# Encoder trunk kernel: a prologue in single token tiles, with the squares of x behind the operand splits

## The chip, the cores and the metric

The kernel runs on one core of a Trainium2 chip. Its time is the device time of one execution, in microseconds (us), and the number that counts is the median of several executions. A trace comes from one further execution under the hardware profiler. The engines are named as in the profile: PE is TensorE (PEld its weight load), DVE is VectorE, ACT is ScalarE, POOL is GpSimd, SP is SyncE, the engine that issues every DMA here. Each engine works through its own instructions in order and waits on semaphores for the others.

## The reference

Two layers over 1088 token rows (a prompt of 1024 and a sample of 64) with a width of 1024. The part that the change touches is the head of the first layer: an RMS norm and the projection `w_in`.

```python
def rmsnorm(x, g):
    xf = x.astype(jnp.float32)
    xf = xf * lax.rsqrt(jnp.mean(xf * xf, axis=-1, keepdims=True) + RMS_EPS)
    return xf.astype(x.dtype) * g
...
    z = rmsnorm(x, norm_g) @ w_in
...
    x = x + mixed @ lp['w_out']
    y, conv_state = conv_ffn(x, lp['ffn_norm'], lp['w_up'], lp['conv_w'], lp['conv_b'], lp['w_down'], conv_buf)
    x = x + y
```

Between them stand three mixers (a gated MLP, a windowed attention and a matrix memory), behind them a convolutional feed-forward block; all of this is the same before and after the change.

## The kernel before

**Tiles.** x lies in HBM by rows of tokens. `TOK` cuts it into nine token tiles: 0 to 7 are 128 prompt rows each, 8 is the sample. `CH` groups three of them into a chunk: 384, 384 and 322 columns once x is turned. On chip x is held turned, as `xT` (128 partitions by 8 blocks of the width by tokens). Every fp32 product is made of three products of a split operand: `split3` (lines 321 to 325) multiplies high by high, low by high and high by low. So x times the norm's gain is split into `actH` (ACT, `norm_high`, line 434) and `actL` (DVE, `norm_low`, line 440), and the weights into `wzH` (ACT) and `wzL` (DVE), `split_wz0`, lines 1397 and 1993, in four pieces of 512 KB: pieces 0 and 1 are the halves of weight group 0, pieces 2 and 3 of group 1.

**The norm's factor comes late.** The products run on x times the gain alone. The factor of each token, `rt`, is applied when ACT takes a finished unit out of PSUM (`evac_z`, line 1429, with the Gelu function). `rt` comes from three steps: ACT squares a tile of x with a running sum (`xsq`, line 1389, semaphore `vs_r`), DVE scales the sums of three tiles (`norm_mean`, line 394), and POOL raises them to the power of -1/2 (`norm_power`, line 400, semaphore `rt_r`).

**The prologue.** SP issues the loads in one row: ident, x tiles 0 to 2, five small rows of gains (`grows`), weight pieces 0 and 1, x tile 3, piece 2, x tile 4, piece 3, then the other tiles. Tiles 7 and 8 share a buffer with 0 and 1, and wait for `vs_r` of those. PE does 12 transposes that feed nobody (`fill`), turns tiles 0 to 2 (`turn_x`, line 882; 8 transposes each), turns the gains, and does 28 more fills. ACT and DVE each copy half of a turned tile to `xT` (lines 1391 and 1988, semaphores `xin_ea` and `xin_ev`). ACT squares each tile before it copies its half. Then come the splits of chunk 0.

**The units.** PE then works through units of `z_products`: a unit is one token tile by 256 columns of `w_in`, 24 matmuls. Unit 0 is tile 0 with group 0, units 1 and 2 are tiles 1 and 2 with group 0, unit 3 is tile 0 with group 1. Behind units 0, 1 and 2 PE turns tiles 3, 4 and 5, behind 4, 5 and 6 the tiles 6, 7 and 8. Since all tiles from 3 on use the same PSUM banks 4 and 5, the turn of tile t waits until both halves of tile t - 1 have been copied out (`xin_ea` and `xin_ev` at least t). ACT's order there is: evacuate unit 0, square and copy tile 3, evacuate unit 1, square and copy tile 4, and so on.

```python
                if t >= 3:
                    pe.wait_ge(xin_ea, t)
                    pe.wait_ge(xin_ev, t)
...
                    act.wait_ge(rt_r, norm_at(2 * l, t // 3) + 1)
                    act.activation(zst[0:r, u % 3, 0:w], bank[z_bank(u)][0:r, 0:w],
                                   ACT.Gelu if u < 18 else ACT.Copy, scale=rt[0:r, t:t + 1]).then_inc(z_ev, 1)
```

Of the kernel before, what the change touches and what calls it, by code (L numbers as in the profile page):

```python
# [7 lines left out]
F32 = mybir.dt.float32  # L8
F32R = mybir.dt.float32r
ALU = mybir.AluOpType  # L10
ACT = mybir.ActivationFunctionType
# [3 lines left out]
P = 128  # L15
D = 1024
KT = D // P
# [12 lines left out]
TOK = [(i * P, P) for i in range(NB)] + [(SOFF, DEC)]  # L30
# [58 lines left out]
def build(nc, I, O):  # L89
# [11 lines left out]
    with ctx:  # L101
# [4 lines left out]
        xT = sb("xT", [P, KT, TC])  # L106
# [224 lines left out]

        def act_at(n, c):

            return n // 2 * 32 + (24 if n % 2 else c * KT)

        def ms_at(n, c):
            return n * 4 + (1, 2, 4)[c]
# [46 lines left out]
        def norm_mean(dve, n, c):  # L384
            if n == 2 * DEPTH and c == 2:
                src = vs[:, 0:3]
            elif n:
                dve.wait_ge(ssq_mm, norm_at(n - 1, c) + 1)
                src = sum_bank(n, c)[:, SS:SS + 3]
            else:  # L390
                dve.wait_ge(vs_r, 3 * c + 3)
                src = vs[:, 3 * c:3 * c + 3]
            k = 2 if c == 2 else 3
            dve.tensor_scalar(ms[:, 3 * c:3 * c + k], src[:, 0:k], 1.0 / D, EPS, ALU.mult, ALU.add).then_inc(ms_r, 1)
            if c == 2:
                dve.tensor_scalar(ms[0:DEC, NB:NB + 1], src[0:DEC, 2:3], 1.0 / D, EPS, ALU.mult, ALU.add).then_inc(ms_r, 1)
# [35 lines left out]
        def norm_high(act, n, c, m):  # L432
            t0, w = CH[c]
            act.activation(actH[:, m, t0:t0 + w], xT[:, m, t0:t0 + w], ACT.Copy,
                           scale=gains[:, n * KT + m:n * KT + m + 1]).then_inc(act_h, 1)

        def norm_low(dve, n, c, m):
            t0, w = CH[c]
# [153 lines left out]
        def _(sp):  # L592
# [3 lines left out]
            def load_x(t):  # L596
                if t >= 7:
                    sp.wait_ge(xin_tp, t - 6)
                    sp.wait_ge(vs_r, t - 6)
                sp.dma_start(xin[0:TOK[t][1], t % 7], I["x_sample"][0] if t == NB else xp[t]).then_inc(xin_in[t % 7], 16)  # L600

            def load_wz(l, s, piece=None):

                g = z_group(s)
                w = ZG[1] if g == 8 else ZG[0]
                k0, k1 = (0, KT) if piece is None else (4 * piece, 4 * piece + 4)
                w_in = I["w_in"][l].rearrange("(k p) n -> p k n", p=P)
                sp.dma_start(rawz(s, l)[:, k0:k1, 0:w], w_in[:, k0:k1, g * ZG[0]:g * ZG[0] + w]).then_inc(
                    rz_in if piece is None else rz0_in[2 * s + piece], 16)

            for t in range(3):
                load_x(t)
            for n, (name, l) in enumerate([(f"{part}_norm", l) for l in range(DEPTH) for part in ("attn", "ffn")]):
                sp.dma_start(grows[n * KT:(n + 1) * KT, :], I[name][l].rearrange("(a b) -> a b", b=P)).then_inc(rows_in, 16)
            sp.dma_start(grows[2 * DEPTH * KT:, :], I["final_norm"].rearrange("(a b) -> a b", b=P)).then_inc(rows_in, 16)
            load_wz(0, 0, 0)
            load_wz(0, 0, 1)
            load_x(3)
            load_wz(0, 1, 0)
# [250 lines left out]
        def _(pe):  # L870
            pe.wait_ge(const_in, 16)

            def turn_x(t):

                r = TOK[t][1]
                b = 2 * t if t < 3 else 4
                pe.wait_ge(xin_in[t % 7], 16 * (t // 7 + 1))
# [3 lines that stand above are left out]
                for k in range(KT):  # L881
                    m = pe.transpose(bank[b + k // 4][:, (k % 4) * P:(k % 4) * P + r],
                                     xin[0:r, t % 7, k * P:(k + 1) * P], ident[0:r, 0:r])
                m.then_inc(xin_tp, 1)

            def fill(count):

                for _ in range(count):
                    pe.transpose(bank[6][:, 0:P], ident[:, :], ident[:, :])

            fill(12)
            for t in range(3):
                turn_x(t)
            n = (2 * DEPTH + 1) * KT
            pe.wait_ge(rows_in, (2 * DEPTH + 1) * 16)
            pe.transpose(bank[7][:, 0:n], grows[0:n, :], ident[0:n, 0:n]).then_inc(rows_tp, 1)
            fill(28)
            pe.wait_ge(s_ones, 3)

            for l in range(DEPTH):  # L900
                M0, F0 = l * MMS, l * FREES

                def z_products(u):

                    s, _, w, t = z_unit(u)
                    t0, r = TOK[t]
                    if u >= 18:
                        pe.wait_ge(wz_l, l * 16 + wz_at(s))
                    if u < 4:
                        if l:  # L910
                            pe.wait_ge(bank_free, l * FREES - 7 + u)
                    elif u < ZB + 2:
                        pe.wait_ge(z_ev, l * ZU + u - 3)
                    else:
                        pe.wait_ge(z_ev, l * ZU + u - 1)
                    if u in (6, 12):
                        pe.wait_ge(act_l, act_at(2 * l, u // 6) + KT)
                    out = bank[z_bank(u)][0:r, 0:w]
                    for k in range(KT):
                        if u in (0, 3) and k % 4 == 0:  # L920
                            pe.wait_ge(wz_l, l * 16 + 2 * s + k // 4 + 1)
                        if u == 0:
                            pe.wait_ge(act_l, act_at(2 * l, 0) + k + 1)
                        m = split3(pe, out, actH[:, k, t0:t0 + r], actL[:, k, t0:t0 + r],
                                   wzH[s % 2][:, k, 0:w], wzL[s % 2][:, k, 0:w], k == 0, k == KT - 1)
                    m.then_inc(z_mm, 1)
# [453 lines left out]

        @block.scalar
        def _(act):
            def turn_x(t):
                t0, r = TOK[t]
                b = 2 * t if t < 3 else 4
                act.wait_ge(xin_in[t % 7], 16 * (t // 7 + 1))
                if t:
                    act.wait_ge(vs_r, t)
                act.activation(xsq[0:r, :], xin[0:r, t % 7], ACT.Square, accum_out=vs[0:r, t:t + 1]).then_inc(vs_r, 1)
                act.wait_ge(xin_tp, t + 1)  # L1390
                act.activation(xT[:, 0:4, t0:t0 + r], bank[b][:, :].rearrange("p (k t) -> p k t", k=4)[:, :, 0:r],
                               ACT.Copy).then_inc(xin_ea, 1)

            def split_wz0(l, j):
                s, k = j // 2, 4 * (j % 2)
                act.wait_ge(rz0_in[j], (l + 1) * 16)
                act.activation(wzH[s][:, k:k + 4, 0:ZG[0]], rawz(s, l)[:, k:k + 4, 0:ZG[0]], ACT.Copy).then_inc(wz_h, 1)

            for t in range(3):
                turn_x(t)  # L1400
            act.wait_ge(rows_tp, 1)
            act.activation(gains[:, :], bank[7][:, 0:(2 * DEPTH + 1) * KT], ACT.Copy).then_inc(gains_r, 1)
            act.wait_ge(gains_r, 1)
            act.wait_ge(xin_ea, 3)
            act.wait_ge(xin_ev, 3)
            for m in range(KT):
                norm_high(act, 0, 0, m)
                if m in (1, 3):
                    split_wz0(0, m // 2)
            split_wz0(0, 2)  # L1410
            split_wz0(0, 3)

            for l in range(DEPTH):
                M0, F0 = l * MMS, l * FREES
# [568 lines left out]
        def _(dve):  # L1983
            def turn_x(t):
                t0, r = TOK[t]
                b = 2 * t if t < 3 else 4
                dve.wait_ge(xin_tp, t + 1)
                dve.tensor_copy(xT[:, 4:8, t0:t0 + r], bank[b + 1][:, :].rearrange("p (k t) -> p k t", k=4)[:, :, 0:r]).then_inc(xin_ev, 1)

            def split_wz0(l, j):  # L1990
                s, k = j // 2, 4 * (j % 2)
                dve.wait_ge(wz_h, l * 16 + j + 1)
                dve.tensor_tensor(wzL[s][:, k:k + 4, 0:ZG[0]], rawz(s, l)[:, k:k + 4, 0:ZG[0]],
                                  wzH[s][:, k:k + 4, 0:ZG[0]].bitcast(F32), ALU.subtract).then_inc(wz_l, 1)

            dve.memset(xT[:, :, SEQ:SOFF], 0.0)
            for c in range(3):
                for t in range(3 * c, 3 * c + 3):
                    turn_x(t)
                if c == 0:  # L2000
                    dve.wait_ge(s_ones, 3)
                    dve.wait_ge(gains_r, 1)
                norm_mean(dve, 0, c)
                for m in range(KT):
                    norm_low(dve, 0, c, m)
                    if c == 0 and m in (1, 3):
                        split_wz0(0, m // 2)
                if c == 0:
                    split_wz0(0, 2)
                    split_wz0(0, 3)  # L2010

            for l in range(DEPTH):
                M0, F0 = l * MMS, l * FREES
# [556 lines left out]
```

## Time and profile before

| | us |
|---|---|
| median of 3 executions | 2484.2 (2484.17 to 2485.09) |
| the profiled execution | 2480.56 |
| its span, first to last instruction | 2478.7 |

The span is cut into the busy time of each engine, the waits (idle time of an engine, put down to what ended it), and the chain of work that ended last, which is followed back from the last instruction. The profiled execution is 3.6 us shorter than the median of the others; what lies around its span is 1.9 us. A timeline merges instructions that follow each other into one row, with their count; one that ends with a bracket tells how long the engine was idle before it and what ended that.

### The profile page before, as it was taken

How to read it: one execution, taken by the hardware profiler on the slowest of the kernel's cores; microseconds unless marked ns; L12 is line 12 of the kernel's file. 1: busy time of each engine (PE TensorE's matmuls, PEld its weight loads, DVE VectorE, ACT ScalarE, POOL GpSimd, SP SyncE). 2: the span in 40 equal slices, each digit the busy share in tenths (PEclk: the TensorE clock that was granted, in tenths of full speed). 3: DMA queues.
4: the chain of work that ended last, by engine and by line, in shares of the span. 5: the costliest groups of instructions: out<-in, count | busy, mean ns of one | idle time of the engine just before them, and what ended most of it. 6: DMA issues, size and time to landing. Idle time of an engine off the chain costs nothing.

```text
span 2478.7 us, 41939 instructions
## 1 busy us (share of the span) xinstructions
PE 2442.6 (99%) x16587; PEld 2377.1 (96%) x16587; DVE 1603.5 (65%) x2715; ACT 1096.6 (44%) x2069; POOL 537.1 (22%) x498
## 2 busy tenths in 40 slices
PE   9999999999999999999999999999999999999999
PEld 8999888999999999999999988889999999999999
DVE  3115688888888887464611266879888888864554
ACT  6325656543433333343433356655343333333453
POOL 0001253432222220010110112444322222200110
PEclk9999999999999999999999999999999999999999
DMA  4443322122222223654524333212122222245564
GB/s 153 132 133 95 114 82 77 54 64 68 79 73 75 79 65 112 199 170 162 196 71 143 110 109 115 82 49 71 62 78 75 73 79 66 74 155 180 176 193 149
DMA packets 238071, 265.89 MB, mean 107 GB/s; under 512 B 15638, under 2 KB 207924, under 8 KB 235700
## 3 DMA queue, kind: packets, MB, share of 16 engines
q1 hardware_dynamic: 237876, 263.22, 33.4%
q8 instruction: 132, 2.16, 0.4%
q14 instruction: 63, 0.52, 0.1%
HBM read 213.06 MB, written 50.11 MB: 106 GB/s over the span
## 4 chain that ended last, share of the span: by engine, by line
PE 88%; DVE 5%; issue 3%; ACT 2%; DMA 1%; POOL 0%; SPq 0%; DVEq 0%; POOLq 0%; ACTq 0%
PE bank L323 27%; PE bank L325 26%; PE bank L324 26%; PE bank L1042 2%; PE bank L1115 1%; PE bank L1084 1%; PE bank L1100 1%; PE bank L1125 1%; PE bank L1064 1%; PE bank L1076 0%; DVE actL L2239 0%; PE bank L995 0%; DMA rawB<-in_w_down 0%; DVE cv L2342 0%; DVE tL L2239 0%
## 5 line engine op out<-in xcount | busy, mean ns | idle before, releaser
L323 PE MATMUL bank<-actH,wb 128*128 128x384 f32 (+1 forms) x1768 | 578.5, 327 | 1.7 <-DVE xT L2036 1.7
L324 PE MATMUL bank<-actL,wb 128*128 128x384 f32 (+1 forms) x1768 | 573.0, 324 | 0.0
L325 PE MATMUL bank<-actH,wb 128*128 128x384 f32 (+1 forms) x1768 | 572.5, 324 | 0.0
L323 PE MATMUL bank<-wzH,actH 128*128 128x256 f32 (+3 forms) x1296 | 369.2, 285 | 2.2 <-DVE actL L440 1.1
L325 PE MATMUL bank<-wzH,actL 128*128 128x256 f32 (+3 forms) x1296 | 364.2, 281 | 0.0
L324 PE MATMUL bank<-wzL,actH 128*128 128x256 f32 (+3 forms) x1296 | 363.8, 281 | 0.0
L323 PEld LDWEIGHTS bank<-actH,wb 128*128 128x128 f32 x1768 | 332.9, 188 | 7.1 <-issue 6.1
L324 PEld LDWEIGHTS bank<-actL,wb 128*128 128x128 f32 x1768 | 333.7, 189 | 0.7
L325 PEld LDWEIGHTS bank<-actH,wb 128*128 128x128 f32 x1768 | 333.8, 189 | 0.0
L323 PEld LDWEIGHTS bank<-wzH,actH 128*128 128x128 f32 (+1 forms) x1296 | 236.3, 182 | 5.1 <-issue 3.0
L323 PE MATMUL bank<-tH,wb 128*128 128x384 f32 x704 | 236.6, 336 | 1.2 <-ACT vn L1788 1.2
L324 PEld LDWEIGHTS bank<-wzL,actH 128*128 128x128 f32 (+1 forms) x1296 | 236.5, 182 | 0.0
L324 PE MATMUL bank<-tL,wb 128*128 128x384 f32 x704 | 236.3, 336 | 0.0
L325 PE MATMUL bank<-tH,wb 128*128 128x384 f32 x704 | 236.3, 336 | 0.0
L325 PEld LDWEIGHTS bank<-wzH,actL 128*128 128x128 f32 (+1 forms) x1296 | 236.1, 182 | 0.0
L1681 ACT ACTIVATE cv<-upb,convc 128x1090 f32<-128x1090 f32 x88 | 114.5, 1301 | 246.3 <-DVE upb L2329 246.1
L2352 DVE TENSOR_TENSOR wb<-raw,wb 128x1024 fp32r<-128x1024 f32 x88 | 107.7, 1224 | 168.5 <-ACT wb L1697 168.3
L2307 DVE TENSOR_TENSOR upb<-bank,upb 128x384 f32<-128x384 f32 x294 | 155.4, 552 | 65.1 <-PE bank L325 62.1
L1659 ACT ACTIVATE Sx<-Sf 128x512 fp32r<-128x512 f32 x168 | 105.3, 628 | 207.8 <-POOL Sf L1952 207.8
L1952 POOL TENSOR_TENSOR Sf<-raw 128x512 f32<-128x512 f32 x84 | 116.6, 1388 | 359.4 <-PE bank L325 355.9
L1429 ACT ACTIVATE zst<-bank,stat 128x256 f32<-128x256 f32 (+3 forms) x162 | 75.8, 472 | 240.1 <-PE bank L325 239.8
L1697 ACT ACTIVATE wb<-raw 128x1024 fp32r<-128x1024 f32 x88 | 93.1, 1060 | 197.5 <-PE bank L325 159.8
(303 smaller groups left out, 5066.6 us busy)
## 6 DMA issues: line engine op xcount, KB each, us to landing
raw<-in_w_up SPq DMA_DIRECT2D x88, 512.0 KB, 4.2
raw<-in_w_down SPq DMA_DIRECT2D x88, 512.0 KB, 3.6
g_scratch<-cv SPq DMA_DIRECT2D x44, 545.0 KB, 3.2
rawz<-in_w_in SPq DMA_DIRECT2D x22, 1024.0 KB, 5.4
zb<-z_scratch SPq DMA_DIRECT2D x16, 1156.0 KB, 5.6
tHf<-g_scratch SPq DMA_DIRECT2D x88, 192.0 KB, 3.6
z_scratch<-zst SPq DMA_DIRECT2D x128, 128.0 KB, 1.7
raw<-in_w_out SPq DMA_DIRECT2D x128, 128.0 KB, 2.9
```

Source lines behind the costliest of these rows:

```text
L323: pe.matmul(out, aH, bH, start=first, stop=False)
L324: pe.matmul(out, aH, bL, start=False, stop=False)
L325: return pe.matmul(out, aL, bH, start=False, stop=last)
L1042: m = pe.matmul(bank[2 * c + p // 2][64 * v:64 * v + 64, (p % 2) * 256 + k0:(p % 2) * 256 + k1], bqT[64 * v:64 * v + 64, p, 64 * c:64 * c ...
L1064: pe.matmul(bank[6][:, 0:4 * r], ones[0:r, :], dA[0:r, 0:4 * r], start=True, stop=True).then_inc(S["A_r"], 1)
L1429: act.activation(zst[0:r, u % 3, 0:w], bank[z_bank(u)][0:r, 0:w], ACT.Gelu if u < 18 else ACT.Copy, scale=rt[0:r, t:t + 1]).then_inc(z_ev, 1)
L1659: act.activation(Sx[:, s, 0], Sf[:, s, 1], ACT.Copy).then_inc(s_h, 1)
L1681: act.activation(cv[:, :], (upb2 if h else upb1)[:, PAD:], ACT.Identity, scale=convc[:, f + 88:f + 89], bias=convc[:, f + 132:f + 133]).th ...
L1697: act.activation(h, t, ACT.Copy).then_inc(w_h, 1)
L1952: pool.tensor_tensor(Sf[:, s, 1], x, y, ALU.add if s == 0 else ALU.subtract).then_inc(s_r, 1)
L2307: dve.tensor_tensor(out, bank[b][:, 0:out.shape[1]], other, ALU.mult if i in (6, 9) else ALU.add).then_inc(take_r, 1)
L2352: dve.tensor_tensor(lo, t, h.bitcast(F32), ALU.subtract).then_inc(w_l, 1)
```

## The change

The prologue is written anew in single tiles. The layers' loops are as they were.

- SP: x tile 0, then the gains, then weight piece 0, then x tiles 1 and 2, then piece 1. The rest follows as before.
- PE: turns tile 0, then the gains, 8 fills, tiles 1 and 2, 4 fills. Unit 0 waits for the low parts of tile 0 alone, unit 1 for those of tiles 1 and 2.
- ACT and DVE: the split of x comes in 8 instructions on the 128 columns of tile 0 (`FIRST`) and 8 on the 256 columns of tiles 1 and 2 (`OTHERS`), where it was 8 on 384 columns. The copies of tiles 1 and 2 and the splits of weight pieces 0 and 1 stand between them.
- ACT: the squares of tiles 0, 1 and 2 stand behind all splits, where each stood ahead of its tile's copy. DVE's `norm_mean` of chunk 0 stands behind the splits too.
- `act_at` counts eight increments more, since chunk 0 has 16 splits now.

```diff
--- before.py
+++ after.py
@@ -331,7 +331,7 @@
 
         def act_at(n, c):
 
-            return n // 2 * 32 + (24 if n % 2 else c * KT)
+            return KT + n // 2 * 32 + (24 if n % 2 else c * KT)
 
         def ms_at(n, c):
             return n * 4 + (1, 2, 4)[c]
@@ -434,6 +434,17 @@
             act.activation(actH[:, m, t0:t0 + w], xT[:, m, t0:t0 + w], ACT.Copy,
                            scale=gains[:, n * KT + m:n * KT + m + 1]).then_inc(act_h, 1)
 
+        FIRST, OTHERS = slice(0, P), slice(P, 384)
+
+        def first_high(act, m, cols):
+
+            act.activation(actH[:, m, cols], xT[:, m, cols], ACT.Copy, scale=gains[:, m:m + 1]).then_inc(act_h, 1)
+
+        def first_low(dve, m, cols):
+            dve.wait_ge(act_h, (KT if cols is OTHERS else 0) + m + 1)
+            dve.scalar_tensor_tensor(actL[:, m, cols], xT[:, m, cols], gains[:, m:m + 1], actH[:, m, cols].bitcast(F32),
+                                     ALU.mult, ALU.subtract).then_inc(act_l, 1)
+
         def norm_low(dve, n, c, m):
             t0, w = CH[c]
             dve.wait_ge(act_h, act_at(n, c) + m + 1)
@@ -608,12 +619,13 @@
                 sp.dma_start(rawz(s, l)[:, k0:k1, 0:w], w_in[:, k0:k1, g * ZG[0]:g * ZG[0] + w]).then_inc(
                     rz_in if piece is None else rz0_in[2 * s + piece], 16)
 
-            for t in range(3):
-                load_x(t)
+            load_x(0)
             for n, (name, l) in enumerate([(f"{part}_norm", l) for l in range(DEPTH) for part in ("attn", "ffn")]):
                 sp.dma_start(grows[n * KT:(n + 1) * KT, :], I[name][l].rearrange("(a b) -> a b", b=P)).then_inc(rows_in, 16)
             sp.dma_start(grows[2 * DEPTH * KT:, :], I["final_norm"].rearrange("(a b) -> a b", b=P)).then_inc(rows_in, 16)
             load_wz(0, 0, 0)
+            load_x(1)
+            load_x(2)
             load_wz(0, 0, 1)
             load_x(3)
             load_wz(0, 1, 0)
@@ -889,12 +901,14 @@
                     pe.transpose(bank[6][:, 0:P], ident[:, :], ident[:, :])
 
             fill(12)
-            for t in range(3):
-                turn_x(t)
+            turn_x(0)
             n = (2 * DEPTH + 1) * KT
             pe.wait_ge(rows_in, (2 * DEPTH + 1) * 16)
             pe.transpose(bank[7][:, 0:n], grows[0:n, :], ident[0:n, 0:n]).then_inc(rows_tp, 1)
-            fill(28)
+            fill(8)
+            turn_x(1)
+            turn_x(2)
+            fill(4)
             pe.wait_ge(s_ones, 3)
 
             for l in range(DEPTH):
@@ -919,7 +933,9 @@
                     for k in range(KT):
                         if u in (0, 3) and k % 4 == 0:
                             pe.wait_ge(wz_l, l * 16 + 2 * s + k // 4 + 1)
-                        if u == 0:
+                        if u == 0 and l == 0:
+                            pe.wait_ge(act_l, k + 1)
+                        elif u == 1 - min(l, 1):
                             pe.wait_ge(act_l, act_at(2 * l, 0) + k + 1)
                         m = split3(pe, out, actH[:, k, t0:t0 + r], actL[:, k, t0:t0 + r],
                                    wzH[s % 2][:, k, 0:w], wzL[s % 2][:, k, 0:w], k == 0, k == KT - 1)
@@ -1380,13 +1396,18 @@
 
         @block.scalar
         def _(act):
-            def turn_x(t):
-                t0, r = TOK[t]
-                b = 2 * t if t < 3 else 4
+            def square_x(t):
+                r = TOK[t][1]
                 act.wait_ge(xin_in[t % 7], 16 * (t // 7 + 1))
                 if t:
                     act.wait_ge(vs_r, t)
                 act.activation(xsq[0:r, :], xin[0:r, t % 7], ACT.Square, accum_out=vs[0:r, t:t + 1]).then_inc(vs_r, 1)
+
+            def turn_x(t):
+                t0, r = TOK[t]
+                b = 2 * t if t < 3 else 4
+                if t > 2:
+                    square_x(t)
                 act.wait_ge(xin_tp, t + 1)
                 act.activation(xT[:, 0:4, t0:t0 + r], bank[b][:, :].rearrange("p (k t) -> p k t", k=4)[:, :, 0:r],
                                ACT.Copy).then_inc(xin_ea, 1)
@@ -1396,19 +1417,28 @@
                 act.wait_ge(rz0_in[j], (l + 1) * 16)
                 act.activation(wzH[s][:, k:k + 4, 0:ZG[0]], rawz(s, l)[:, k:k + 4, 0:ZG[0]], ACT.Copy).then_inc(wz_h, 1)
 
-            for t in range(3):
-                turn_x(t)
+            turn_x(0)
             act.wait_ge(rows_tp, 1)
             act.activation(gains[:, :], bank[7][:, 0:(2 * DEPTH + 1) * KT], ACT.Copy).then_inc(gains_r, 1)
+            split_wz0(0, 0)
             act.wait_ge(gains_r, 1)
+            act.wait_ge(xin_ea, 1)
+            act.wait_ge(xin_ev, 1)
+            for m in range(4):
+                first_high(act, m, FIRST)
+            turn_x(1)
+            for m in range(4, KT):
+                first_high(act, m, FIRST)
+            split_wz0(0, 1)
+            turn_x(2)
             act.wait_ge(xin_ea, 3)
             act.wait_ge(xin_ev, 3)
             for m in range(KT):
-                norm_high(act, 0, 0, m)
-                if m in (1, 3):
-                    split_wz0(0, m // 2)
+                first_high(act, m, OTHERS)
             split_wz0(0, 2)
             split_wz0(0, 3)
+            for t in range(3):
+                square_x(t)
 
             for l in range(DEPTH):
                 M0, F0 = l * MMS, l * FREES
@@ -1994,20 +2024,28 @@
                                   wzH[s][:, k:k + 4, 0:ZG[0]].bitcast(F32), ALU.subtract).then_inc(wz_l, 1)
 
             dve.memset(xT[:, :, SEQ:SOFF], 0.0)
-            for c in range(3):
+            turn_x(0)
+            dve.wait_ge(s_ones, 3)
+            dve.wait_ge(gains_r, 1)
+            split_wz0(0, 0)
+            for m in range(4):
+                first_low(dve, m, FIRST)
+            turn_x(1)
+            for m in range(4, KT):
+                first_low(dve, m, FIRST)
+            split_wz0(0, 1)
+            turn_x(2)
+            for m in range(KT):
+                first_low(dve, m, OTHERS)
+            split_wz0(0, 2)
+            split_wz0(0, 3)
+            norm_mean(dve, 0, 0)
+            for c in range(1, 3):
                 for t in range(3 * c, 3 * c + 3):
                     turn_x(t)
-                if c == 0:
-                    dve.wait_ge(s_ones, 3)
-                    dve.wait_ge(gains_r, 1)
                 norm_mean(dve, 0, c)
                 for m in range(KT):
                     norm_low(dve, 0, c, m)
-                    if c == 0 and m in (1, 3):
-                        split_wz0(0, m // 2)
-                if c == 0:
-                    split_wz0(0, 2)
-                    split_wz0(0, 3)
 
             for l in range(DEPTH):
                 M0, F0 = l * MMS, l * FREES
```

On ACT, from its split of chunk 0 to the copy of x tile 3. Before (`rz0_in2` and `rz0_in3` are the landings of weight pieces 2 and 3, `z_mm` is a finished unit):

```order
L434 ACTIVATE actH<-xT,gains 128x384 [waits xin_ev,xin_ea,gains_r]
L434 ACTIVATE actH<-xT,gains 128x384
L1397 ACTIVATE wzH<-rawz 128x4x256 [waits rz0_in0]
L434 ACTIVATE actH<-xT,gains 128x384 x2
L1397 ACTIVATE wzH<-rawz 128x4x256 [waits rz0_in1]
L434 ACTIVATE actH<-xT,gains 128x384 x4
L1397 ACTIVATE wzH<-rawz1a 128x1024 [waits rz0_in2]
L1397 ACTIVATE wzH<-rawz1a 128x1024 [waits rz0_in3]
L1429 ACT_TABLE_LOAD [waits rt_r]
L1429 ACTIVATE zst<-bank,stat 128x256 [waits z_mm]
L1389 ACTIVATE xsq,stat<-xin 128x1024 [waits vs_r,xin_in3]
L1391 ACTIVATE xT<-bank 128x4x128 [waits xin_tp]
```

and after, on ACT, from the split of weight piece 1:

```order
L1418 ACTIVATE wzH<-rawz 128x4x256 [waits rz0_in1]
L1412 ACTIVATE xT<-bank 128x4x128 [waits xin_tp]
L441 ACTIVATE actH<-xT,gains 128x256 [waits xin_ev,xin_ea]
L441 ACTIVATE actH<-xT,gains 128x256 x7
L1418 ACTIVATE wzH<-rawz1a 128x1024 [waits rz0_in2]
L1418 ACTIVATE wzH<-rawz1a 128x1024 [waits rz0_in3]
L1404 ACTIVATE xsq,stat<-xin 128x1024 [waits xin_in0]
L1404 ACTIVATE xsq,stat<-xin 128x1024 [waits vs_r,xin_in1]
L1404 ACTIVATE xsq,stat<-xin 128x1024 [waits vs_r,xin_in2]
L1459 ACT_TABLE_LOAD [waits rt_r]
L1459 ACTIVATE zst<-bank,stat 128x256 [waits z_mm]
L1404 ACTIVATE xsq,stat<-xin 128x1024 [waits vs_r,xin_in3]
```

The three squares of chunk 0 have moved from the front of ACT's row to the place between the last weight split and the table load of unit 0's evacuation.

On DVE, the same place in the program. Before:

```order
L1988 COPY xT<-bank 128x4x128 [waits xin_tp] x3
L394 TENSOR_SCALAR stat<-stat 128x3 [waits vs_r,gains_r,s_ones]
L440 SCALAR_TENSOR_TENSOR actL<-xT,gains,actH 128x384 [waits act_h] x2
L1993 TENSOR_TENSOR wzL<-rawz,wzH 128x4x256 [waits wz_h]
L440 SCALAR_TENSOR_TENSOR actL<-xT,gains,actH 128x384 [waits act_h] x2
L1993 TENSOR_TENSOR wzL<-rawz,wzH 128x4x256 [waits wz_h]
L440 SCALAR_TENSOR_TENSOR actL<-xT,gains,actH 128x384 [waits act_h] x4
L1993 TENSOR_TENSOR wzL<-rawz1a,wzH 128x1024 [waits wz_h] x2
```

and after:

```order
L2018 COPY xT<-bank 128x4x128 [waits xin_tp]
L2023 TENSOR_TENSOR wzL<-rawz,wzH 128x4x256 [waits wz_h,gains_r,s_ones]
L445 SCALAR_TENSOR_TENSOR actL<-xT,gains,actH 128x128 [waits act_h] x4
L2018 COPY xT<-bank 128x4x128 [waits xin_tp]
L445 SCALAR_TENSOR_TENSOR actL<-xT,gains,actH 128x128 [waits act_h] x4
L2023 TENSOR_TENSOR wzL<-rawz,wzH 128x4x256 [waits wz_h]
L2018 COPY xT<-bank 128x4x128 [waits xin_tp]
L445 SCALAR_TENSOR_TENSOR actL<-xT,gains,actH 128x256 [waits act_h] x8
L2023 TENSOR_TENSOR wzL<-rawz1a,wzH 128x1024 [waits wz_h] x2
L394 TENSOR_SCALAR stat<-stat 128x3 [waits vs_r]
```

DVE's copies of tiles 1 and 2, which stood together ahead of every split, now each wait behind a split of weights or of x, and `norm_mean` (line 394) has gone from the front to the end.

## Rows read from the trace of the kernel before

**Rows 1.** The page: the span, and PE's busy time, share and instructions.
```profile
span 2478.7 us, 41939 instructions
PE 2442.6 (99%) x16587; PEld 2377.1 (96%) x16587; DVE 1603.5 (65%) x2715; ACT 1096.6 (44%) x2069; POOL 537.1 (22%) x498
```

**Rows 2.** Timeline of PE, first units and turns: start us, us, line, operation, tiles.
```profile
16.64 0.36 PE L323 MATMUL bank<-wzH,actH 128*128 128x256 f32 x1 [1.12 <-DVE actL L440]
...
18.60 1.03 PE L882 MATMUL bank<-ident,xin 128*128 128x128 f32 x8
...
22.30 1.04 PE L882 MATMUL bank<-ident,xin 128*128 128x128 f32 x8
```

**Rows 3.** Timeline of ACT, from the first copy to the copy of x tile 3.
```profile
6.67 0.60 ACT L1391 ACTIVATE xT<-bank 128x512 f32<-128x512 f32 x1 [1.01 <-PE bank L882]
...
10.20 0.21 ACT L1402 ACTIVATE gains<-bank 128x40 f32<-128x40 f32 x1
...
16.40 1.99 ACT L1397 ACTIVATE wzH<-rawz1a 128x1024 fp32r<-128x1024 f32 x2
18.41 1.28 ACT L1429 ACT_TABLE_LOAD   x1
19.70 0.47 ACT L1429 ACTIVATE zst<-bank,stat 128x256 f32<-128x256 f32 x1
20.07 1.05 ACT L1389 ACTIVATE xsq<-xin 128x1024 f32<-128x1024 f32 x1
21.02 0.19 ACT L1389 ACTIVATION_READ_ACCUMULATOR xsq<-xin 128x1 f32 x1
21.11 0.59 ACT L1391 ACTIVATE xT<-bank 128x512 f32<-128x512 f32 x1
```

**Rows 4.** Timeline of SP: the issues of the first loads.
```profile
1.19 1.37 SPq L600 DMA_DIRECT2D xin<-in_x_prompt  x3
...
4.02 0.29 SPq L615 DMA_DIRECT2D grows<-in_final_norm  x1
4.35 0.95 SPq L608 DMA_DIRECT2D rawz<-in_w_in  x2
```

**Rows 5.** DMA issues, us to landing: x tile 0, weight pieces 0 and 1.
```profile
xin<-in_x_prompt SPq DMA_DIRECT2D x1, 512.0 KB, 3.3
...
rawz<-in_w_in SPq DMA_DIRECT2D x1, 512.0 KB, 5.6
...
rawz<-in_w_in SPq DMA_DIRECT2D x1, 512.0 KB, 6.5
```

**Rows 6.** Timeline of ACT: eight high parts at 384 and at 322 columns.
```profile
30.27 4.15 ACT L434 ACTIVATE actH<-xT,gains 128x384 fp32r<-128x384 f32 x8
...
44.41 3.74 ACT L434 ACTIVATE actH<-xT,gains 128x322 fp32r<-128x322 f32 x8
```

**Rows 7.** Timeline of DVE: a weight split, and the copy of a tile.
```profile
14.74 1.22 DVE L1993 TENSOR_TENSOR wzL<-rawz,wzH 128x1024 fp32r<-128x1024 f32 x1
...
20.27 0.69 DVE L1988 COPY xT<-bank 128x512 f32<-128x512 f32 x1
```

**Rows 8.** Timeline of three engines: from the last square of chunk 1 to its factor.
```profile
27.53 0.19 ACT L1389 ACTIVATION_READ_ACCUMULATOR xsq<-xin 128x1 f32 x1
...
27.75 0.17 DVE L394 TENSOR_SCALAR stat<-stat 128x3 f32<-128x3 f32 x1
...
28.00 0.85 POOL L400 TENSOR_TENSOR stat<-stat 128x3 f32<-128x3 f32 x1 [16.32 <-DVE stat L394]
```

**Rows 9.** Waits of PE, longest first: what for, us in total, times, longest.
```profile
PE bank L323 <- DVE Sx L2235: 8.5, 2, 4.3
```

**Rows 10.** Stretches around the first of them: length, PE busy (instructions), granted clock, DMA share, GB/s.
```profile
514.00:516.00 2.00, 0.00 (x0) 1.00 0.00 0
516.00:518.00 2.00, 0.23 (x1) 0.96 0.00 0
...
519.00:520.00 1.00, 1.00 (x5) 0.50 0.07 16
...
521.00:522.00 1.00, 1.00 (x6) 0.87 0.00 0
522.00:523.00 1.00, 1.00 (x8) 1.00 0.00 0
```

## Prediction

> **What bounds the kernel now.** I read the page first: PE is busy for 99% of the span [rows 1]. So the time is PE's work plus its few waits, and an edit of the prologue can only move the point from which PE runs without a stop. That point is read from PE's timeline. Its last wait of the prologue ends at 16.64 us, where unit 0 had waited for low parts of x, and from there units and turns follow each other: tile 3 is turned at 18.60, tile 4 at 22.30 [rows 2]. Unit 0 is thus done at 18.60 and unit 1 at 22.30. The row at 22.30 is my yardstick: whatever the change does ahead of it, everything behind it is the same work in the same order on every engine, so the kernel's time moves by as much as that row moves (plus what the clock adds, below).
>
> Two things must be there for the turn of tile 4. One is PE itself, done with units 0 and 1. The other is ACT: it must have copied tile 3, and ahead of that copy stand, in its order, all splits, the table load, the evacuation of unit 0 and the square of tile 3. ACT's timeline shows that chain before: splits to 18.39, table load at 18.41, evacuation at 19.70, square at 20.07, its sum at 21.02, copy at 21.11, done at 21.70 [rows 3]. The slack against PE's 22.30 was only 0.6 us. That is the number to look at, since the change puts work on this chain.
>
> **The gain on PE's side.** Tile 0's own splits are smaller and stand first, so unit 0 can be done earlier. I build the times below: unit 0 ends near 16.5 instead of 18.60, and unit 1 waits for the `OTHERS` parts and ends near 19.5 instead of 22.30. By this alone 2.8 us would be won.
>
> **ACT's chain after the change, step by step.**
> - Start. The first square used to run while PE turned tile 0. Now ACT has nothing before the copy at 6.67 [rows 3], since fills and tile 0 come as before. Copy and gains take 0.5 and 0.2: 7.4.
> - Weight piece 0. Its issue stood at 4.35, behind two tiles of x [rows 4], and it landed 5.6 later, at 9.95 [rows 5]. Now it follows tile 0 and five small issues, near 3.4. With little ahead of it it should take tile 0's 3.3 [rows 5]: 6.7, at most a us more. I take a start of 7.4, one split's pitch is 1.0 (two in 1.99, [rows 3]): 8.4.
> - Tile 0's high parts. Eight at 384 columns took 4.15, 0.52 each, eight at 322 took 3.74, 0.47 each [rows 6]: 0.83 ns for a column, so 0.31 at 128 columns and 0.41 at 256. Four: 9.6. Copy of tile 1, 0.5: 10.1 (its turn is done by then if it lands by 9; two of 512 KB stand ahead of it). Four more: 11.3.
> - Weight piece 1 had landed at 4.80 + 6.5 = 11.3 [rows 4, 5]; four tiles of 512 KB stand ahead of it now as then, with a pause in the issues for the gains. I take 11.5, up to 12.2. High part: 12.55.
> - Now the cross wait. ACT must wait for DVE's copy of tile 2 (`xin_ev`), which stands behind DVE's split of piece 1. That takes 1.14 to the next instruction's start (1.22 long), the copy 0.69 [rows 7]: 12.6 + 1.14 + 0.69 = 14.45.
> - `OTHERS`, eight at 0.41: 17.75. Pieces 2 and 3, 1.95: 19.7. So the splits are done 1.3 later than before, though they began sooner: sixteen instructions cost 5.8 where eight cost 4.15, and ACT stands still for about 1.5 at the cross wait.
> - The three squares. Square and sum take 1.14 (20.07 to 21.21, [rows 3]), and each waits for the sum before it: 3 x 1.17 = 3.5, to 23.2. Before, all this was at the front, where half of it was hidden by PE's transposes.
> - The factor. From the end of the last sum to the factor's end took 27.72 to 28.85, 1.13, through DVE and POOL [rows 8]: 24.35. Before, nobody waited for it. Now the table load has the wait on `rt_r` ahead of it, so it starts only then: 1.29 to the evacuation's start [rows 3], 25.65. Then as before 1.41 from the evacuation to the copy's start and 0.59 for the copy [rows 3]: 27.65.
>
> So the turn of tile 4 starts at 27.7, and 27.7 - 22.3 = **5.4 us later**. PE's gain is eaten entirely: PE would stand still from 19.5 to 27.7. Queued behind the same wait are, on SP, the loads of tiles 7 and 8, which wait for `vs_r`; they would leave near 21 and are turned after 40, so they cost nothing. DVE's `norm_mean` holds up its copy of tile 3, but only to 24, less than ACT's.
>
> **The clock.** The trace has a stall of such a size: PE idle for 4.3 us, for DVE's Sx [rows 9]. Around its end the granted clock falls to half, that is from 2.4 to 1.2 GHz. The stretches give 0.04 x 2 x 2 = 0.16, three full microseconds, and 0.26: 3.4 us at the lower level [rows 10]. At half rate these do 1.7 us of work, and by instructions (5 a us against 8) the loss is 1.3. A stall of 8 us is longer than that, so I expect it again, and take 1.6. From both sides: nothing if the clock stays, and twice the 1.3, 2.7, if PE starts at the lower level and has to work through a second such stretch. The waits of 1.1 us in the prologue of before show no such price [rows 2], but a stall of 8 us is near to the one of 4.3, not to those.
>
> Sum: 5.4 + 1.6 = +7.0. The profiled execution would go from 2480.56 to 2487.6; against the median of 2484.2, which is 3.6 above it, the same difference gives **2491.2**. A shift as a whole is right because no engine behind unit 2 has work that waits for anything but this chain.
>
> The switch of ACT's table is where a page speaks. In the row the load takes 1.28, and the evacuation starts 0.01 behind it. The Trainium skill (ScalarE: Activation LUTs, What ACT_TABLE_LOAD costs) gives about 1.28 us for the load and another 1.38 for a drain. By it, an estimate from that page, the sum would be 1.4 higher, since the switch is now on the path; the trace shows no drain behind the load, and I keep the row's figure.
>
> **Rivals.**
> - *The table load is not held.* If ACT loads the table as soon as the squares are issued, the load lies beside DVE and POOL, and 1.1 of it is saved: +5.9, 2490.1. For it: before, it started 0.02 behind the split. Against: it has the wait on `rt_r`, which had long been met then.
> - *The clock stays.* +5.4, 2489.6. For it: short waits leave it alone. Against: [rows 10].
> - *The table switch costs more.* If ACT has to empty first, with its factor just in, a switch could cost its length twice: +8.3, 2492.5. The row at 19.70 speaks against it.
> - *The other side: PE is what decides.* If ACT's chain came through by 19.5, the turn of tile 4 would start when unit 1 ends, and the kernel would win 2.8: 2481.4. It decides from the point where the copy of tile 3 is done by 19.5; ACT's work alone, from 6.67 on with no wait, is 0.7 + 4 x 1.0 + 5.8 + 2 x 0.5 + 3.5 = 15.0, which ends at 21.7 ahead of the factor, so it needs squares or splits far cheaper than their rows. Between it and the forecast lies the case that waits and splits are cheaper by a us or so in sum and the clock stays: +3 to +5, within 0.2%.
>
> **How the numbers follow.** Forecast as worked out, with steps off by up to a us: 0.64. Load not held: 0.11. Clock stays with the stall as forecast: 0.09. Switch dearer: 0.03. Chain shorter, within 0.2%: 0.10. PE decides: 0.03, also within 0.2%. About 0.2%, 5 us, is what a measurement of this kernel can tell from no change, so the line is at 2489.2. Some of the cases that end above it in the mean (clock stays, load not held) spill over it by 0.03 together. Faster gets 0.01, for what no case covers. That makes faster 0.01, same 0.10 + 0.03 + 0.03 - 0.01 = 0.15, slower 0.84. The range: down to a stall as forecast without the clock's price, 2489.2, and up to piece 1 landing at 12.2 (+0.7) with the clock's dear end (+1.1), 2493.0.
>
> **What the profile after would show.** The turn of tile 4 at 27.7 with an idle time ahead of it of some 8 us, put down to ACT's or DVE's copy; the splits of pieces 2 and 3 done near 19.7; squares from there to 23.2; the factor near 24.4; the table load behind it, not beside it; a granted clock of 0.5 for some 3.4 us around 28. Unit 0 would run in two halves, with a wait for the low part of piece 1 between them. The forecast is wrong if the copy of tile 3 ends before 24, or if the load starts ahead of the factor.

## Result, and the profile after

| | before | after |
|---|---|---|
| median of 7 executions each, us | 2484.17 (2479.72 to 2485.09) | 2491.29 (2489.12 to 2494.29) |
| profiled execution, us | 2480.56 | 2491.29 |
| its span, us | 2478.7 | 2489.5 |

The ratio is 1.0034, with a 95% interval from 1.0023 to 1.0045: the changed kernel is slower by 0.34%, 7.1 us between the medians. The forecast was 2491.2. The profiled executions stand further apart, by 10.8 us (the forecast for the changed kernel's was 2487.6); where these come from is taken up below.

The page of the changed kernel shows the same busy shares, and a first slice (of 62 us) in which PE is no longer busy all the time:

```profile
span 2489.5 us, 41924 instructions
PE 2446.0 (98%) x16571; PEld 2380.9 (96%) x16571; DVE 1602.2 (64%) x2723; ACT 1099.3 (44%) x2077; POOL 537.2 (22%) x498
...
PE   7999999999999999999999999999999999999999
```

The waits of PE over the whole changed kernel (what for, us in total, times, longest) have a new first row. The second is the one that stood first before, [rows 9]:

```profile
PE bank L894 <- ACT xT L1412: 8.7, 1, 8.7
PE bank L323 <- DVE Sx L2273: 8.5, 2, 4.3
```

PE's timeline puts that wait in front of the turn of x tile 4. These rows answer to [rows 2]: the second half of unit 0 starts at 13.74 after its wait for the low part of weight piece 1 (16.64 before, for a low part of x), tile 3 is turned at 15.27 instead of 18.60, tile 4 at 27.79 instead of 22.30. The 8 transposes take 1.94 us instead of 1.04, and tile 5 is turned at 33.91, which is 6.1 behind tile 4.

```profile
13.74 0.39 PE L323 MATMUL bank<-wzH,actH 128*128 128x256 f32 x1 [0.95 <-DVE wzL L2023]
15.27 1.04 PE L894 MATMUL bank<-ident,xin 128*128 128x128 f32 x8
27.79 1.94 PE L894 MATMUL bank<-ident,xin 128*128 128x128 f32 x8 [8.65 <-ACT xT L1412]
33.91 1.03 PE L894 MATMUL bank<-ident,xin 128*128 128x128 f32 x8
```

ACT's timeline of the same stretch answers to [rows 3]. It can be read from the bottom: the copy of tile 3 at 27.10 is behind its square (26.07), that behind the evacuation of unit 0 (25.69), that behind the table load (24.40), that behind the factor (POOL, a wait of 1.29), and that behind three squares from 19.50 on:

```profile
12.33 0.58 ACT L1412 ACTIVATE xT<-bank 128x512 f32<-128x512 f32 x1
14.38 3.31 ACT L441 ACTIVATE actH<-xT,gains 128x256 fp32r<-128x256 f32 x8 [1.47 <-DVE xT L2018]
17.60 1.99 ACT L1418 ACTIVATE wzH<-rawz1a 128x1024 fp32r<-128x1024 f32 x2
19.50 1.04 ACT L1404 ACTIVATE xsq<-xin 128x1024 f32<-128x1024 f32 x1
...
22.92 0.19 ACT L1404 ACTIVATION_READ_ACCUMULATOR xsq<-xin 128x1 f32 x1
24.40 1.28 ACT L1459 ACT_TABLE_LOAD   x1 [1.29 <-POOL stat L400]
25.69 0.47 ACT L1459 ACTIVATE zst<-bank,stat 128x256 f32<-128x256 f32 x1
26.07 1.05 ACT L1404 ACTIVATE xsq<-xin 128x1024 f32<-128x1024 f32 x1
...
27.10 0.59 ACT L1412 ACTIVATE xT<-bank 128x512 f32<-128x512 f32 x1
```

The stretches of the changed kernel (length, PE busy, granted clock) show what the stall did to TensorE's clock. It fell to half, that is from 2.4 to 1.2 GHz, while PE was idle, and came back only between 32 and 34 us, some 5 us after PE had work again:

```profile
22.00:24.00 2.00, 0.00 (x0) 0.68 0.78 270
24.00:26.00 2.00, 0.00 (x0) 0.50 0.32 98
...
28.00:30.00 2.00, 2.00 (x11) 0.50 0.19 66
30.00:32.00 2.00, 2.00 (x11) 0.50 0.00 0
32.00:34.00 2.00, 2.00 (x15) 0.76 0.00 0
34.00:36.00 2.00, 2.00 (x20) 1.00 0.20 66
```

A landmark further down is ACT's next table load, behind unit 17. It stands at 72.81 before (the first row) and at 80.73 after (the second), 7.9 later:

```profile
72.81 1.28 ACT L1449 ACT_TABLE_LOAD   x1
80.73 1.28 ACT L1479 ACT_TABLE_LOAD   x1
```

The later turn of tile 4 makes 5.5 of it (27.79 - 22.30). The other 2.4 I put down to the clock; the first experiment tests that. I use this landmark for all kernels below, since nothing that the variants edit stands behind it.

### The profile page after: what moved, and what is told of

Read it like the earlier page. It is cut to its first block, busy times and chain, and to the rows that moved or that the text cites. A ratio compares the mean times of both kernels' runs of the same rounds, so it can differ in the third digit from the quotient of the medians.

```text
span 2489.5 us, 41924 instructions
## 1 busy us (share of the span) xinstructions
PE 2446.0 (98%) x16571; PEld 2380.9 (96%) x16571; DVE 1602.2 (64%) x2723; ACT 1099.3 (44%) x2077; POOL 537.2 (22%) x498
## 4 chain that ended last, share of the span: by engine, by line
PE 87%; DVE 6%; issue 3%; ACT 2%; DMA 1%; POOL 1%; SPq 0%; DVEq 0%; POOLq 0%; ACTq 0%
PE bank L323 27%; PE bank L325 26%; PE bank L324 26%; PE bank L1058 1%; PE bank L1131 1%; DMA zb<-z_scratch 1%; PE bank L1100 1%; PE bank L1116 1%; PE bank L1141 1%; DVE hc L2213 1%; DVE actL L2277 1%; PE bank L1080 1%; PE bank L1092 0%; DMA rawB<-in_w_down 0%; PE bank L1011 0%
```

## Experiments

Each was timed beside the kernel before, unless said otherwise, and profiled once. Single profiles differ by some tenths of a us in when x and the weights land (in those of the changed kernel's variants the split of weight piece 0 starts between 7.3 and 8.2), so a share read from two of them is taken as good to about 0.5 us, an estimate from these starts.

**The clock taken out.** 76 transposes that feed nobody, into a bank that is free there, fill PE's wait:

```diff
                     z_products(u)
                     if l == 0:
+                        if u == 1:
+                            fill(76)
                         if u in (0, 1, 2):
                             turn_x(3 + u)
```

> The changed kernel with 76 more fill transposes on PE between unit 1 and the turn of tile 4, at 0.109 us each 8.3 us, inside its wait of 8.65 us. If the clock is what costs beyond the wait: the turn of tile 4 stays at 27.8, no row shows a granted clock of 0.5 there, the turn of tile 5 starts 3.7 us behind that of tile 4 instead of 6.1, and the median is 2.4 us under the changed kernel's, near 2488.9. Rival, that unit 2 was slow for another reason (a port shared with ACT and DVE): the 6.1 us stay and the median is 2491.3.

Measured: PE's timeline has the fills from 19.49 on, and tile 5's turn 3.8 behind tile 4's, instead of 6.1. The last two rows are stretches: with the fills the granted clock stays at 1.00.

```profile
19.49 8.46 PE L901 MATMUL bank<-ident 128*128 128x128 f32 x76
28.30 1.06 PE L894 MATMUL bank<-ident,xin 128*128 128x128 f32 x8 [0.36 <-issue]
32.06 1.04 PE L894 MATMUL bank<-ident,xin 128*128 128x128 f32 x8
...
26.00:28.00 2.00, 1.95 (x18) 1.00 0.19 65
28.00:30.00 2.00, 1.70 (x15) 1.00 0.20 66
```

Tile 4's turn is 0.5 later here, for a first tile and weights that landed later. The landmark is at 78.84, 6.0 behind the kernel before, which is the 6.0 by which tile 4's turn is late (28.30 - 22.30) and nothing for the clock. Median 2489.85, ratio 1.0027 (1.0016 to 1.0037). So the clock's share of the changed kernel is 2.4 us, and the rival of a slow unit 2 is out. The medians don't show it: 2489.85 is 7.2 above the kernel before timed beside it (2482.66), and the changed kernel was 7.1 above its own. The trace is what shows it.

**The squares back in front.** The changed kernel, with each square ahead of its tile's copy, and `norm_mean` ahead of the last weight splits on DVE:

```diff
...
             def turn_x(t):
...
-                if t > 2:
-                    square_x(t)
+                square_x(t)
...
             split_wz0(0, 2)
             split_wz0(0, 3)
-            for t in range(3):
-                square_x(t)
...
+            norm_mean(dve, 0, 0)
             split_wz0(0, 2)
             split_wz0(0, 3)
-            norm_mean(dve, 0, 0)
```

> The changed kernel with each square ahead of its tile's copy again, and norm_mean ahead of the splits of weight pieces 2 and 3; order of loads, splits by tile and fills stay as changed. If the squares and the factor behind the splits make the wait: splits of pieces 2 and 3 done near 20.5, factor long there, table load beside nothing but at once, turn of tile 4 near 23.9 instead of 27.8, median 2485 to 2487.5. Rival, that the doubled number of splits and the wait of ACT for DVE's copy of tile 2 carry most of it: the turn of tile 4 after 26 and a median of 2490.

Measured: ACT's table load follows the splits at once, and PE's turn of tile 4 starts at 23.97.

```profile
18.57 1.99 ACT L1417 ACTIVATE wzH<-rawz1a 128x1024 fp32r<-128x1024 f32 x2
20.58 1.28 ACT L1455 ACT_TABLE_LOAD   x1
...
23.97 1.94 PE L894 MATMUL bank<-ident,xin 128*128 128x128 f32 x8 [3.87 <-ACT xT L1411]
```

Median 2487.51, ratio 1.0018 (1.0009 to 1.0027); landmark at 75.91, 3.1 behind the kernel before. The place of the squares and the factor carries 3.8 of the 5.5 us of the stall, and the rest of the change, with more and smaller splits and the wait for DVE, carries 1.7 of its own (some 0.2 of it is a later start: the split of weight piece 0 is at 7.54 here, at 7.32 in the changed kernel). A wait of 3.9 is enough for the lower clock: the 8 transposes again take 1.94.

**The table load out from behind the factor.** One line behind the third square:

```diff
             for t in range(3):
                 square_x(t)
+            act.preload_act_table_set("gelu_and_others")
```

> The changed kernel with the load of the Gelu table right behind the third square, where it waits for nothing, beside norm_mean and the power. If the load is on the path because it stands behind the wait for the factor: the evacuation of unit 0 starts near 24.5 and the turn of tile 4 near 26.6, 1.15 earlier than 27.8; the median 1.1 us under the changed kernel's (2490.1). Rival, that the load is hidden anyway: the turn of tile 4 at 27.8.

Measured: ACT loads the table while DVE and POOL make the factor.

```profile
23.36 1.28 ACT L1442 ACT_TABLE_LOAD   x1
24.66 0.47 ACT L1460 ACTIVATE zst<-bank,stat 128x256 f32<-128x256 f32 x1
...
26.76 1.94 PE L894 MATMUL bank<-ident,xin 128*128 128x128 f32 x8 [7.38 <-ACT xT L1412]
```

The evacuation follows 0.02 behind the load, and the turn of tile 4 is at 26.76; from the start of the last square to the copy's start it is now 3.87, against 5.14 in the changed kernel. The landmark (79.12) is 1.6 earlier. The load was on the path by its place behind the wait. The median doesn't show it: 2490.95, ratio 1.0032 (1.0019 to 1.0044), where 2490.1 was expected.

**The squares alone.** The kernel before, with nothing but the squares of tiles 0 to 2 and `norm_mean` moved behind the splits:

```diff
...
+            for t in range(3):
+                square_x(t)
...
-                norm_mean(dve, 0, c)
+                if c:
+                    norm_mean(dve, 0, c)
...
                     split_wz0(0, 2)
                     split_wz0(0, 3)
+                    norm_mean(dve, 0, 0)
```

> The kernel before with one part of the change alone: squares of tiles 0 to 2 and norm_mean behind the splits. If the place of the squares makes most of the wait: splits done near 18.0, squares to 21.5, factor 22.7, table load behind it, turn of tile 4 near 26.0 instead of 22.3; +3.7, and up to 2.4 more if the clock falls: 2487.9 to 2490.3. Rival, that the squares merely fill idle time of ACT: the turn of tile 4 stays within 0.5 us of 22.3, 2484.2.

Measured: unit 0 and the turn of tile 3 are about where they were (18.36 against 18.60), and the turn of tile 4 waits.

```profile
22.96 1.28 ACT L1436 ACT_TABLE_LOAD   x1 [1.29 <-POOL stat L400]
...
26.35 1.94 PE L882 MATMUL bank<-ident,xin 128*128 128x128 f32 x8 [4.13 <-ACT xT L1396]
```

Median 2489.95, ratio 1.0028 (1.0018 to 1.0038); landmark at 78.38, 5.6 behind the kernel before. From this side too the move of the squares is worth 4.1 us of stall, and 1.5 for the clock.

**The copies ahead.** If the stall is only for the copies of x, the copies can go first. ACT takes its half of tile 3 ahead of the splits of weight piece 2, tile 4's behind piece 3, tile 5's behind the squares; DVE likewise:

```diff
...
+            turn_x(3)
             split_wz0(0, 2)
             split_wz0(0, 3)
+            turn_x(4)
             for t in range(3):
                 square_x(t)
+            turn_x(5)
...
                         if u in (1, 2, 3):
-                            turn_x(u + 2)
+                            square_x(u + 2)
```

> The changed kernel with the copies of tiles 3, 4 and 5 (both halves) taken out of the row behind the evacuations: tile 3's ahead of the splits of weight piece 2, tile 4's behind those of piece 3, tile 5's behind the squares; their squares stay where they were. If the wait is for the copy alone: the turn of tile 4 starts when unit 1 is done, near 19.3, with no wait of 8 us and no half clock. Then ACT is late next: unit 4 waits for the first evacuation near 27.3, and the turn of tile 7 for the copy of tile 6, behind chunk 1's high parts, near 38 (36.41 in the kernel before). Median 1 to 2 us over the kernel before: 2484 to 2485. Rival, that PE's gain comes through: the turn of tile 7 near 33.5 and a median near 2480.

Measured: the 8.65 us are gone, and ACT is late at the next two places, as PE's timeline shows. The last row is the turn of tile 7 in the kernel before.

```profile
19.36 1.06 PE L894 MATMUL bank<-ident,xin 128*128 128x128 f32 x8
...
27.69 0.39 PE L323 MATMUL bank<-wzH,actH 128*128 128x256 f32 x1 [0.74 <-ACT zst L1462]
...
37.87 1.39 PE L894 MATMUL bank<-ident,xin 128*128 128x128 f32 x8 [3.36 <-ACT xT L1412]
...
36.41 1.06 PE L882 MATMUL bank<-ident,xin 128*128 128x128 f32 x8
```

The landmark is at 75.81, 3.0 late: 1.5 for tile 7's turn (37.87 against 36.41) and the rest for a clock that fell again 0.6 us behind the end of that wait (granted 0.73 in 38 to 39 us, 0.50 in 39 to 41), which I had not expected. The median, 2488.81, and the ratio, 1.0020 (1.0011 to 1.0029), are above what I gave (2484 to 2485). In this profile 5.7 us more were lost behind the landmark (the span is 2487.4, 8.7 above before). How much of that belongs to the kernel and how much to this one execution isn't shown.

**ACT's whole order.** As the last, with the table loaded early, and with the evacuations and chunk 1's high parts ahead of the squares of tiles 3 to 8:

```diff
...
+                        if u in (4, 9):
...
                             for m in range(KT):
                                 norm_high(act, 0, u // 4, m)
+                        if u == 4:
+                            turn_x(6)
                     evac_z(u)
+                    if l == 0:
+                        if u == 4:
+                            square_x(3)
+                        if u == 5:
+                            square_x(4)
+                            turn_x(7)
+                            square_x(5)
...
```

> As the kernel with the copies ahead, and the Gelu table loaded behind the third square, the evacuations of units 0 to 3 and chunk 1's high parts ahead of the squares of tiles 3 to 8, which follow the evacuations of units 4 to 7; norm_mean of chunks 1 and 2 behind chunk 1's low parts. If only ACT's order stood in the way: no wait of PE over 1 us behind unit 0, the turn of tile 7 near 33.3 instead of 36.41, and 3 us under the kernel before: near 2480. Rival, that ACT's work in sum binds up to unit 12: the 3 us are lost again before 60 us.

Measured: one wait is left behind unit 0, of 1.09, for DVE's copy of tile 6, which stood behind all of chunk 1's low parts:

```profile
35.28 1.06 PE L894 MATMUL bank<-ident,xin 128*128 128x128 f32 x8 [1.09 <-DVE xT L2031]
```

The landmark is at 71.69, 1.1 ahead of the kernel before, not 3. Median 2483.67, not near 2480; ratio 1.0002 (0.9993 to 1.0011).

A second version puts both copies of tile 6 behind the fifth part of chunk 1:

> As the kernel with all of ACT's order changed, but both copies of tile 6 stand behind the fifth part of chunk 1 instead of the eighth, since the turn of tile 7 waited 1.09 us there for DVE's. If that copy alone was late: the turn of tile 7 follows unit 5 without a wait, near 34.2, 2.2 us ahead of the kernel before (36.41), and unit 6 waits for the last low parts by less than 0.5. The median would be 1 us under that of the version before it, near 2482, which is under what can be told from the kernel before; the trace decides. Rival: the wait moves to unit 6, for the low parts, and the turn of tile 8 stays at 39.1.

Measured: tile 7 is turned at 34.02 without a wait, unit 6 then waits 0.22 for a low part, and the landmark is at 70.85.

```profile
34.02 1.03 PE L894 MATMUL bank<-ident,xin 128*128 128x128 f32 x8
35.27 0.35 PE L323 MATMUL bank<-wzH,actH 128*128 128x256 f32 x1 [0.22 <-DVE actL L451]
```

So the single-tile prologue can be 2.0 us ahead of the old one at 70 us, and 2.4 ahead at the turns of tiles 4 (19.85) and 7, once the copies of x no longer queue on ACT behind the squares, the factor and the first evacuation. It started late in this profile: ACT waited 0.71 for weight piece 0 to land. In the whole it doesn't show: 2484.45 against 2485.35 beside it, ratio 0.9998 (0.9989 to 1.0007). No version beats the kernel before by what can be told.

**Is it the change, or when things fall?** The profiled executions of the kernel before and the changed one differ by 10.8 us, 2.9 more than the landmark. Both kernels stop twice for DVE's Sx, for 4.3 us each time [rows 9], but what follows isn't the same. The stretches below are of the kernel before and of the changed one, 40 us around the first such stop and 35 around the second, with the same wait in them:

```profile
500.00:540.00 40.00, 35.00 (x204) 0.96 0.22 67
1730.00:1765.00 35.00, 30.14 (x169) 0.95 0.20 62
```

```profile
500.00:540.00 40.00, 35.59 (x197) 0.91 0.13 42
1730.00:1765.00 35.00, 30.75 (x175) 0.90 0.19 60
```

A mean of 0.96 over 40 us is some 3.4 us at half clock, 0.91 some 7. To see whether the change does this, I only delayed the kernel before, by more fills ahead of unit 0 (one execution each):

```diff
-            fill(28)
+            fill(68)
```

> The kernel before with 40 more fills ahead of unit 0 (4.4 us, of which some 1.1 come through). Nothing else is moved. If the granted clock behind the two late stalls for Sx depends on where in time they fall, its stretch of 0.5 (3.4 us before, 6.8 in the changed kernel) can take either length here. If it depends on what the change does, it is 3.4.

> The kernel before with 56 more fills ahead of unit 0 (6.1 us, of which some 2.9 come through). As for the kernel with 40 more: either length of the stretch at a granted clock of 0.5 if it depends on where the stalls fall, 3.4 if it depends on the change.

Measured: with 68 fills the landmark is 1.2 late and the first stop has the long stretch, the second the short one. With 84 it is 3.2 late and both have the long one. These are the two rows with 68, and then the two with 84:

```profile
500.00:540.00 40.00, 35.64 (x203) 0.91 0.23 68
1730.00:1765.00 35.00, 30.13 (x169) 0.95 0.25 76
```

```profile
500.00:540.00 40.00, 35.64 (x202) 0.91 0.21 64
1730.00:1765.00 35.00, 30.75 (x173) 0.90 0.25 76
```

The stop for Sx is 4.3 us in all of them. So the longer stretch isn't a mark of the change. The spans are 2480.7 and 2485.5, 2.0 and 6.8 over that of before: a plain delay of 3.2 can come out as 6.8. One execution of each doesn't say how often.

What the stretch behind the second stop is worth can be read from the row that ends that stop, here in the kernel before and in the changed one:

```profile
1738.93 0.44 PE L323 MATMUL bank<-tH,Sx 128*128 128x384 f32 x1 [4.24 <-DVE Sx L2235]
1748.06 0.69 PE L323 MATMUL bank<-tH,Sx 128*128 128x384 f32 x1 [4.25 <-DVE Sx L2273]
```

The changed kernel is 9.1 late there and 10.8 at the end: of the 2.9, 1.2 arise up to this row and 1.7 behind it. In all six profiles in which the second stretch is the long one (a mean of 0.90), 1.6 to 1.8 us more are lost behind this row than in the kernel before. Of the four others with a short one (0.95), three lose 0 to 0.2, and that of the squares back in front 1.2. The kernel with the copies ahead has two short stretches; its 5.7 us were lost ahead of this row, for a reason that stays open.

## Why the prediction was right

- **The yardstick.** The turn of tile 4 was taken as the point that everything behind it follows, and that held as far as the landmark: 5.5 and 2.4 make the 7.9 at 80.73. Behind it the same work doesn't take the same time: all ten other profiles lose more there than that of the kernel before, by 0.8 to 5.7 us, and the changed kernel by 2.9. In part that is the yardstick itself, since the profiled execution of the kernel before is 3.6 us under its median.
- **PE's side.** Unit 1 was to end near 19.5 and ended near 19.1 (27.79 - 8.65); unit 0 was expected near 16.5 and was done at 15.3. Both earlier than forecast, and worth nothing.
- **ACT's chain.** Step by step, forecast and measured: weight piece 0's split at 7.4 and 7.32; piece 1's at 11.5 and 11.38; the cross wait's end at 14.45 and 14.38; splits done at 19.7 and 19.5; squares done at 23.2 and 23.1; factor at 24.35 and 24.3; evacuation at 25.65 and 25.69; copy done at 27.65 and 27.7. The wait for DVE's copy was 1.47, forecast about 1.5.
- **The landings.** Piece 0 was issued at 3.41 and had landed by 7.32, 3.9 later, where 3.3 was taken, with up to one more allowed; the copy of the gains was done at 7.2, so ACT waited 0.1 for it.
- **The table load** stood behind the factor, and took 1.29 to the evacuation. Between the end of the load and the next row of ACT lies 0.01 to 0.02, in the changed kernel and in every variant. The Trainium skill (ScalarE: Activation LUTs, What ACT_TABLE_LOAD costs) adds a drain of about 1.38; the trace doesn't agree.
- **The clock** was the term that was mis-sized: 1.6 forecast, 2.4 measured, inside the bound of 2.7. The cost was read from one stop, for Sx, behind which PE worked for 3.4 us at half clock; here it worked for 5.2 us at it (27.79 to about 33.0). The variants show that this is the length to price: PE worked for 3.0, 3.1, 3.9 and 5.2 us at half clock with the squares in front, the squares alone, the table early and the changed kernel, and the landmark lost 1.4, 1.5, 1.9 and 2.4 us beyond the turn of tile 4, a little under half of it each time.
- **Why the median met the forecast** to 0.1 us: in part by luck. The shift up to the landmark is 7.9 and the medians stand 7.1 apart, while the profiled execution, forecast at 2487.6, came at 2491.29. Beside the variants the kernel before had medians of 2482.7 twice and 2485.4 once. The interval, 5.7 to 11.2 us, holds 7.0 and 7.9.
- **The range.** Its foot was said to be the stall without the clock's price. That sum gives 2489.6; 2489.2 is the line of 0.2%.
- **The rivals.** "The table load is not held" and "PE is what decides" are ruled out by the rows above, "the table switch costs more" by the 0.01 behind the load, and "the clock stays" by the granted clock. Only by changing the order on ACT did PE's side come to decide, and then it gave 2.0 us in the trace, where it had been priced at 2.8.

## What to carry to other kernels

Moving a step off the front of an engine's row doesn't take it off the path: look for the first instruction behind its new place that a busier engine waits for, and count all that now stands ahead of it, waits on semaphores and table loads included. Here a slack of 0.6 us on ACT decided over a gain of 2.8 us on PE. And where a stall of TensorE grows from nothing to several us, price the slower clock after it as well, by the time that TensorE works at it.

## What was not expected of the hardware

- A stop of the same length (4.3 us) was followed by 3.4 us at half clock in one profile and by some 7 in another, and kernels that differ only by idle fills at the front show both. The same kernel's executions lie up to 6.4 us apart (2479.2 to 2485.5 in 21), which may come from this in part; that wasn't shown.
- The granted clock fell during waits of 3.9, 4.1 and 8.65 us, and just behind one of 3.4. The price doesn't follow the wait's length: 1.5 us for 4.1 (of the 5.6 at the landmark, 4.1 are the turn of tile 4, 26.35 against 22.30) and 2.4 for 8.65. It follows the time that PE still works at half clock, 3.1 and 5.2 us in these two.
